# A two-layer trunk step on one core: the first feed-forward projection run tile by tile as its shift and scale columns are computed, with activations and vectors laid out on the host

## What is computed

```python
mod = (silu(cond) @ w_mod[layer] + b_mod[layer]).reshape(-1, 9, 1024)      # 9 vectors of 1024 for each of 2 conditions
# first sub-layer: shift = mod[:,0], scale = mod[:,1], gate = mod[:,2]
h = x * rsqrt(mean(x*x) + 1e-6) * norm_g[0] * (1 + scale) + shift          # cond = c_ctx for context, c for latent
x = x + 0.5 * gate * ((silu(h @ w_gate) * (h @ w_up)) @ w_out)             # FFN width 2816
...                                                                       # mixer, FFN, FFN, mixer, FFN
return x of the context tokens, x of the latent tokens, new_cache_k, new_cache_v
```

## Time and profile before

| | |
|---|---|
| median of 3 runs | 1500.81 us (1499.41 to 1501.71) |
| the profiled execution | 1499.5 us |
| its span | 1497.7 us |
| PE busy, of the span | 94% |
| first matmul of the first projection | 45.47 us |
| start of unit 2 | 67.53 us |
| end of the first FFN's matmuls | about 325.4 us |
| last residual done | about 1489.9 us |

### The profile page before, as it was taken

One profiled execution on the slowest core, in us unless ns is written; L12 is line 12 of the kernel. 1 busy time (PEld: TensorE's weight loads), 2 busy tenths in 40 slices (PEclk: granted clock), 3 DMA queues, 4 the chain that ended last, 5 costly groups with the idle time before them and its releaser, 6 DMA issues.

```text
span 1497.7 us, 21193 instructions
## 1 busy us (share of the span) xinstructions
PE 1407.8 (94%) x8134; PEld 1375.4 (92%) x8134; DVE 970.0 (65%) x1394; ACT 557.7 (37%) x731; POOL 122.5 (8%) x110
## 2 busy tenths in 40 slices
PE   5799999989866899999998999999989989999998
PEld 3799999989845799999998999999989989999998
DVE  2777678968998566666757666679763477444332
ACT  2433332237666443333224333332345343333221
POOL 1000000014555100000001000000021010000000
PEclk9899999989878999999998999999989999999999
DMA  8765655752200235555652555547523325433421
GB/s 325 261 231 176 203 177 200 285 182 96 86 32 29 102 133 201 188 191 174 234 181 85 197 193 185 193 149 295 219 99 134 126 85 186 137 122 130 141 84 42
DMA packets 45114, 242.96 MB, mean 162 GB/s; under 512 B 4997, under 2 KB 6889, under 8 KB 24328
## 3 DMA queue, kind: packets, MB, share of 16 engines
q1 hardware_dynamic: 44464, 241.99, 46.7%
q10 hardware_dynamic: 600, 0.30, 0.1%
HBM read 240.57 MB, written 1.70 MB: 162 GB/s over the span
## 4 chain that ended last, share of the span: by engine, by line
PE 83%; DVE 10%; DMA 2%; ACT 2%; issue 1%; POOL 1%; ACTq 0%; SPq 0%; DVEq 0%; POOLq 0%
PE ps L1185 27%; PE ps L1186 27%; PE ps L1187 27%; DVE conv L974 4%; DVE w_lo L790 1%; DMA conv_rows<-in_conv_w 1%; DVE n_full L876 1%; PE ps L1254 1%; DVE m_raw L812 1%; DVE smax L1039 1%; ACT w_hi L528 1%; DVE a_lo L883 0%; POOL n_acc L453 0%; DMA m_raw<-in_w_pairs 0%; PE ps L1554 0%
## 5 line engine op out<-in xcount | busy, mean ns | idle before, releaser
L1185 PE MATMUL ps<-a_hi,w_hi 128*128 128x384 f32 x1744 | 591.7, 339 | 19.1 <-DVE a_lo L883 14.0
L1186 PE MATMUL ps<-a_lo,w_hi 128*128 128x384 f32 x1744 | 588.5, 337 | 0.0
L1187 PE MATMUL ps<-a_hi,w_lo 128*128 128x384 f32 x1744 | 588.1, 337 | 0.0
L790 DVE TENSOR_TENSOR w_lo<-w_raw,w_hi 128x2048 fp32r<-128x2048 f32 x153 | 352.9, 2306 | 162.3 <-ACT w_hi L528 162.0
L528 ACT ACTIVATE w_hi<-w_raw 128x2048 fp32r<-128x2048 f32 x153 | 292.1, 1909 | 264.7 <-PE ps L1187 200.2
L1185 PEld LDWEIGHTS ps<-a_hi,w_hi 128*128 128x128 f32 x1744 | 332.1, 190 | 23.4 <-issue 10.0
L1186 PEld LDWEIGHTS ps<-a_lo,w_hi 128*128 128x128 f32 x1744 | 332.1, 190 | 0.1
L1187 PEld LDWEIGHTS ps<-a_hi,w_lo 128*128 128x128 f32 x1744 | 331.7, 190 | 0.0
L812 DVE SCALAR_TENSOR_TENSOR m_raw<-m_raw 128x1024 f32<-128x1024 f32 x252 | 296.0, 1220 | 1.0 <-ACT m_raw L589 1.0
L1187 PE MATMUL ps<-h_hi,w_lo 128*128 (+1 forms) x704 | 236.6, 336 | 0.0
L1186 PE MATMUL ps<-h_lo,w_hi 128*128 (+1 forms) x704 | 236.6, 336 | 0.0
(11 more groups left out here) (179 smaller groups left out, 666.2 us busy)
## 6 DMA issues: line engine op xcount, KB each, us to landing
w_raw<-in_w_units SPq DMA_DIRECT2D x153, 1024.0 KB, 5.0
m_raw<-in_w_rows SPq DMA_DIRECT2D x126, 512.0 KB, 3.6
m_raw<-in_w_pairs SPq DMA_DIRECT2D x9, 1024.0 KB, 7.7
out<-x_nat SPq DMA_DIRECT2D x3, 512.0 KB, 3.1
x_nat<-in_x_sample SPq DMA_DIRECT2D x1, 1024.0 KB, 12.5
fourier<-in_k_fourier SPq DMA_DIRECT2D x1, 768.0 KB, 4.4
x_nat<-in_x_prompt SPq DMA_DIRECT2D x1, 512.0 KB, 10.7
m_raw<-in_c_ctx SPq DMA_DIRECT2D x1, 512.0 KB, 5.7
```

Of the source, the lines that this page charges most:

```text
L790: nc.vector.tensor_tensor(w_lo[:, slot(u), :], w_raw[:, slot(u), :], w_hi[:, slot(u), :].bitcast(FP32), ALU.subtract).then_inc(lo_done, 1)
L1185: mm(out, whi, mhi, start=start, stop=False)
L1186: mm(out, whi, mlo, start=False, stop=False)
L1187: return mm(out, wlo, mhi, start=False, stop=stop)
```

## The change

The host now lays out `x` (as `x_cols`, channels on partitions), the two conditions (`cond_cols`), and all bias and norm vectors (`cols_a`, `cols_b`, `conv_cols`), and transposes the output back (`y_cols`). The transposes on PE and their copies go, at the start and at the end. A pair of modulation columns now holds one tile of shift and the same tile of scale, so pair `k` is all that channel tile `k` needs. There are 8 pairs in place of 9, pairs 3 to 7 in buffers of their own (`p_raw`), all loaded with no wait. After tiles 0 and 1, PE interleaves: pair `k + 2`, then channel tile `k` of units 0 and 1 together (12 matmuls), then the columns of pair `k + 2`. Two more modulation tiles are left to DVE, in the output units.

```diff
-FIRST_TILES = MRING * GROUPS_FIRST * PAIR_TILES
+FIRST_TILES = KT * PAIR_TILES
-TILES_OUT = {0: [3, 3] + [2] * 8, ...
+TILES_OUT = {0: [3] * 4 + [2] * 6, ...
 # SP, start
-            sp.dma_start(ident[:], k_ident).then_inc(const_in, 16)
-            sp.dma_start(cond_rows[0:KT, :], c_ctx...); sp.dma_start(cond_rows[KT:2 * KT, :], c[0]...)
-            for b in range(MRING):
-                load_pair(0, b)
-            sp.dma_start(x_nat[:, 0, :], x_prompt[0]); sp.dma_start(x_nat[:, 1:TT, :], x_sample[0]...)
+            sp.dma_start(cond_raw[:], cond_cols).then_inc(cond_in, 16)
+            sp.dma_start(ident[:], k_ident).then_inc(const_in, 16)
+            sp.dma_start(x[:], x_cols).then_inc(x_in, 16)
 # SP, load_ffn(0)
-                    for pair in range(MRING, MRING * GROUPS_FIRST):
-                        if pair == MRING * GROUPS_FIRST - 2:
-                            load_unit(u0)
-                        load_pair(pair // MRING, pair % MRING)
+                    load_pair(0)
+                    load_unit(u0)
+                    load_unit(u0 + 1)
+                    for k in range(1, KT):
+                        load_pair(k)
+                    load_unit(u0 + 2)
+                    sp.wait_ge(mod_used, MRING)        # then the condition rows and the tiles
 # SP, end
-            for tt in range(TT):
-                sp.wait_ge(out_c, tt + 1)
-                sp.dma_start(dst, x_nat[:, tt, :]).then_inc(out_done, 16)
+            for d in range(KT):
+                sp.wait_ge(x_ready, KT * N_SUB + d + 1)
+                sp.dma_start(y_cols[:, d, :], x[:, d, :]).then_inc(out_done, 16)
 # ACT
-            act.wait_ge(cond_t, 1)
+            act.wait_ge(cond_in, 16)
-            for dst, src in ( ... 13 row loads ... (conv_rows[:, :], conv_w[0])):
+            for dst, src in ((vec_a[:], cols_a), (vec_b[:], cols_b), (conv_wt[:], conv_cols)):
                 act.dma_start(dst, src).then_inc(vectors_in, 16)
             norm_stats(0)
-            ...                                        # vec_a, vec_b, conv_wt out of PSUM
             split(0)
-            norm(0)
+            norm(0, 0, 1)
             split(1)
+            norm(0, 1, KT)
 # DVE
+            def part_copy(k):
+                dve.wait_ge(mod_used, k + 1)
+                if k >= 2:
+                    dve.wait_ge(cols_done, k - 1)
+                nc.vector.tensor_copy(mod_part[:, k % 2, :], ps[:, SUM_BANK[k % 2], 0:PAIR]).then_inc(part_copied, 1)
+            def first_modulation(k):
+                dve.wait_ge(cols_done, k + 1)
+                nc.vector.tensor_scalar(m_shift[:, 0, k, :], ps[:, 7, 0:2], vec_a[...], None, ALU.add)
+                nc.vector.tensor_scalar(m_scale[:, 0, k, :], ps[:, 7, 2:4], scale_bias[:, k:k + 1],
+                                        vec_a[...], ALU.add, ALU.mult).then_inc(first_mods, 1)
+            dve.wait_ge(vectors_in, 48)
+            dve.wait_ge(dve_self, mark(nc.vector.tensor_scalar(scale_bias[:], vec_a[...], 1.0, None, ALU.add)))
+            dve.wait_ge(x_in, 16)
+            dve.sem_inc(x_ready, KT)
             part_copy(0)
-            for d in range(KT):
-                dve.wait_ge(x_t, d + 1)
-                nc.vector.tensor_copy(x[:, d, :], ps[:, d % 6, 0:TOK]).then_inc(x_ready, 1)
-            cols_copy(0)
+            first_modulation(0)
             norm_stats(0)
-            part_copy(1); cols_copy(1); split(0); part_copy(2); cols_copy(2); modulation_in(0); norm(0); split(1)
+            dve.wait_ge(bc_done, 1)
+            dve.wait_ge(first_mods, 1)
+            scaled(0, 0)                               # n_full of one tile, the first half of norm()
+            low(0, 0)                                  # a_lo of one tile, the second half
+            split(0)
+            split(1)
+            part_copy(1)
+            first_modulation(1)
+            for k in range(1, KT):
+                dve.wait_ge(first_mods, k + 1)
+                scaled(0, k)
+                if k + 1 < KT:
+                    part_copy(k + 1)
+                low(0, k)
+                if k + 1 < KT:
+                    first_modulation(k + 1)
             ffn(0)
 # PE
+            def mod_sums(k):
+                pe.wait_ge(pair_in[k], 16)
+                if k >= 2:
+                    pe.wait_ge(part_copied, k - 1)
+                ...                                    # 8 matmuls, 128x256 moving, 32 columns each, as before
             pe.wait_ge(cond_ready, 2)
+            mod_sums(0)
+            mod_columns(0)
+            norm_sums(0)
+            norm_spread(0)
+            mod_sums(1)
+            mod_columns(1)
+            for m in range(2):
+                pe.wait_ge(lo_done, RING + m + 1)
+            for k in range(KT):
+                if k + 2 < KT:
+                    mod_sums(k + 2)
+                pe.wait_ge(a_ready, k + 1)
+                for m in range(2):
+                    for h in range(2):
+                        ins = three(ps[:, 2 * m + h, 0:TOK], ..., a_hi[:, k, :], a_lo[:, k, :], k == 0, k == KT - 1)
+                    if k == KT - 1:
+                        ins.then_inc(unit_done, 1)
+                if k + 2 < KT:
+                    mod_columns(k + 2)
             ffn(0)                                     # without its first_units; continues with unit 2
-            ...                                        # at the end: 24 transposes of x; ACT: 3 copies to x_nat
```

More of the change, by code:

```diff
@@ L157, in modulation_pairs, with columns @@
 def modulation_pairs(w_mod):
-    n = MRING * GROUPS_FIRST
-    w = w_mod[0, :, 0:n * PAIR].reshape(KT, P, n, PAIR).transpose(2, 1, 0, 3)
-    return np.ascontiguousarray(w, dtype=np.float32).reshape(n, P, UNIT)
+    w = w_mod[0, :, 0:2 * D_MODEL].reshape(KT, P, 2, KT, P).transpose(3, 1, 0, 2, 4)
+    return np.ascontiguousarray(w, dtype=np.float32).reshape(KT, P, UNIT)
+def columns(*vectors):
+    return np.ascontiguousarray(np.concatenate([np.asarray(v, np.float32).reshape(-1, P) for v in vectors]).T)
 def modulation_rows(w_mod):
@@ L217, in build @@
         n_full = sb("n_full", [P, KT, TOK], stack=r)
[L218 to L221, removed]
+        p_raw = sb("p_raw", [P, KT - MRING, UNIT], stack=r)
         r.close()
@@ L267, in build @@
         unit_done = sem("unit_done")
-        mod_in = [sem(f"mod_in{i}") for i in range(MRING)]
+        pair_in = [sem(f"pair_in{k}") for k in range(KT)]
         mod_used = sem("mod_used")
@@ L540, in norm_stats, with norm @@
                 nc.scalar.activation(stat[:, 4:4 + TT], stat[:, 0:TT], ACT.Sqrt).then_inc(root_done, 1)
-            def norm(n):
-                for d in range(KT):
+            def norm(n, d0=0, d1=KT):
+                for d in range(d0, d1):
                     for cnd, lo, hi in SEGS:
@@ L866, in norm_stats, with scaled, low @@
                                         stat[:, 8:8 + TT].unsqueeze(2).to_broadcast([P, TT, P]), ALU.mult).then_inc(diag_done, 1)
+            def scaled(n, d):
+                for cnd, lo, hi in SEGS:
+                    nc.vector.scalar_tensor_tensor(n_full[:, d, lo:hi], ps[:, BC_BANK[n], lo:hi],
+                                                   m_scale[:, n, d, cnd:cnd + 1], x[:, d, lo:hi],
+                                                   ALU.mult, ALU.mult).then_inc(full_done, 1)
+            def low(n, d):
+                for cnd, lo, hi in SEGS:
+                    dve.wait_ge(a_hi_done, 2 * (KT * n + d) + cnd + 1)
+                    ins = nc.vector.scalar_tensor_tensor(a_lo[:, d, lo:hi], n_full[:, d, lo:hi],
+                                                         m_shift[:, n, d, cnd:cnd + 1],
+                                                         a_hi[:, d, lo:hi].bitcast(FP32), ALU.add, ALU.subtract)
+                ins.then_inc(a_ready, 1)
             def norm(n):
-                bank = BC_BANK[n]
                 dve.wait_ge(bc_done, n + 1)
@@ L1569, in _ @@
             ffn(5)
-            pe.wait_ge(x_ready, KT * (N_SUB + 1))
-            for tt in range(TT):
-                for d in range(KT):
-                    ins = nc.tensor.transpose(ps[:, 2 * tt + d // 4, (d % 4) * P:(d % 4 + 1) * P],
-                                              x[:, d, tt * P:(tt + 1) * P], ident[:])
-                ins.then_inc(out_t, 1)
 FFN_AT = {0: 0, 2: 1, 3: 2, 5: 3}
@@ L1612 @@
     named["w_rows"] = modulation_rows(np.asarray(inputs["w_mod"]))
+    tokens = np.concatenate([np.asarray(inputs["x_prompt"])[0], np.asarray(inputs["x_sample"])[0]])
+    named["x_cols"] = np.ascontiguousarray(tokens.reshape(TOK, KT, P).transpose(2, 1, 0), dtype=np.float32)
+    named["cond_cols"] = columns(inputs["c_ctx"], inputs["c"])
+    vectors = {n: np.asarray(inputs[n]) for n in _VECTORS}
+    named["cols_a"] = columns(vectors["b_mod"][0], vectors["norm_g"])
+    named["cols_b"] = columns(vectors["b_mod"][1], *(vectors[n] for n in _VECTORS[2:7]),
+                              *(np.tile(vectors[n], 2) for n in _VECTORS[7:]))
```

(1 more changed line is left out.)

189 lines of the change are left out of this document (50 added, 139 removed).

## The result

The changed kernel takes 1505.88 us (median of 8 runs, 1504.07 to 1509.38), the kernel before beside it 1501.69 us (8 runs). The ratio is 1.0032, 95% interval 1.0021 to 1.0043: slower by 0.3%, where no change was forecast. The profiled execution's span grew from 1497.7 to 1502.3 us.

A forecast was written before the change was run, and what follows sets the result against it. PE was taken as the bound from unit 2 on, so only unit 2's start and the tail matter. Start 3.8 + clock 1.5 - end 5.2 = +0.1 us, median 1500.81 to 1500.9, range 1494.5 to 1506.

The forecast's parts named there:

- Costed at nothing: Loads ahead of their use, condition rows, and two extra DVE tiles covered in the output units: no cost.
- The bound given for the lost cover: Output units: without cover, the two extra DVE tiles would cost 4.6 us.
- a gap at PE in the output units, which would be the two extra tiles: Listed sign of a wrong forecast: PE waiting in the output units because of DVE's two added tiles; no size given.
- Vectors: Start: all three vector loads landed at 15.7 us, 384 packets at 41 a us on ACT's queue.
- Rival A: Start: vectors arrive early, at best x limits at 8.5, all steps 7.2 us earlier, 1493.7 us; chance 0.20.
- Norm, copy, rounds: Start, after the vectors: squares 16.1, first products 35.9, rounds 3.62 each, last a_hi 58.8, unit 2 at 71.3 us.
- rivals B and C: B: rounds at half clock, up to 19 us more, 0.12; C: late vectors or round waits, from 3.0 us, 0.18.
- Clock: Unit 2, after PE's idle: half clock for 3 us loses 1.5 us, bounds 0 and 3.4.
- rival D: PE's gap before unit 2 leaves clock up, only the end counts: 1499.4 us; chance 0.50 together with the forecast.
- The end: After the last residual: last store lands in 1.9 us, span ends at 1492.5, gain 5.2 us (4.4 to 5.5).
- the 2.45 us of the prediction: Kernel's end: the last store's landing time by the skill's fit, which would make the gain 4.7 us.

The follow-up runs named there:

- experiment 2: Kernel before with two more modulation tiles in the first FFN's output units, two fewer in the second's: 1506.27 us, ratio 1.0024 to the kernel before.
- experiment 1: Changed kernel with its two extra modulation tiles moved from the output units to right after step(0): 1503.39 us, ratio 1.0005 to the kernel before.
- experiment 3: Changed kernel with unit 33 loaded before the first FFN's last two modulation tiles in SP's queue: 1500.29 us, ratio 0.9985 to the kernel before.
- experiment 6: Changed kernel with x released as it lands, DVE waiting first only for vec_a: 1500.36 us, ratio 0.9985 to the kernel before.

## Why the prediction was wrong

**The step that failed** is the one under "Costed at nothing": "The two extra DVE tiles fall in the output units. There the split of unit 26 is done at 260.2 and needed at 267.0". The cover was measured at the split, which indeed stayed early: PE has no gap from unit 2 to 332. It was not measured at the end of DVE's queue, where gate and residuals stand. There DVE had no cover already before: its gate came at 322.36, 3.4 us before the end of PE's last product, with 16 residuals of 0.33 us behind it (5.3 in all), and PE waited 2.31. The bound given for the lost cover, 4.6 us, holds the 3.3 us of the border. The tiles cost 3.6 us alone (experiment 2) and give about 4 back when taken out of the change (experiment 1). Part of the path was not seen at all: the lateness passes through SP's queue, as tile, free buffer, load of unit 33, split, and then the gate (experiment 3). The prediction's list of signs did name this one: "a gap at PE in the output units, which would be the two extra tiles". The gap came just behind those units.

**Vectors.** 15.7 was worked out and 15.77 measured, but that close a match is luck. ACT's queue moved 432 packets from 6 to 16 us, not 384, and 54 a us and not 41 (the rows below):

```profile
q1 hardware_dynamic: 378, 2.74, 93.6%
q10 hardware_dynamic: 378, 0.15, 7.9%
```

(After, 7 to 14 us: packets, MB, share; q1 is SP's queue, q10 ACT's.) With these two figures the prediction's sum, 2.7 + 3.5 + 432/54, would have been 14.2. Rival A was right that full rows go faster than the mean rate of before, and wrong that the vectors would be early by much. The Trainium skill says in "DMA: Bandwidth & Descriptors", section "Queues, rings and completion order", that a DMA engine drains a whole packet of one ring, typically some 9 to 17 descriptors, before it switches. By the prediction's reading of it, the 8 rows of a load on each engine would have gone in one turn. The trace does not agree: the two queues moved 378 packets each in 7 us, one for one, and the counts keep within 3 of each other in single stretches of 0.2 us too (7.2 to 7.8 us: 9 to 10, 11 to 12, 14 to 13). Waiting for all three loads cost 7.0 us by ratio (experiment 6; 5.8 by landmarks), near the 7.2 that the prediction gave rival A at best.

**Norm, copy, rounds.** Squares at 16.06 (16.1), first products at 36.52 (35.9), the five rounds after the first 3.64 each (3.62) without a wait, so rivals B and C are out. The spread took 1.65 in place of 1.35, the copy of pair 1's sums started at 33.24 in place of 32.5, and the first 12 matmuls took 2.93 in place of 2.6. With such tenths the last `a_hi` is at 59.91, 1.1 later than 58.8, and unit 2 at 72.49, 1.2 later than 71.3.

**Clock.** 3.1 us at half clock in unit 2 (windows above), 1.46 us longer to the FFN's end: as sized. (Its upper bound, 3.4 for "twice as long at half", should be 3.0.) So rival D did not come.

**The end** gave 5.56 for 5.2. The last store landed in 1.9 us, as in proportion. The fit in the Trainium skill's "DMA: Bandwidth & Descriptors", section "Anatomy of one DMA", is given there for DMAs that GpSimd issues, and SP issues these stores, so the 2.45 us of the prediction stretched it, and the trace does not agree with it.

**In sum**, +0.1 was forecast. With 3.3 for the border and 1.2 for the start it would have been +4.6. The measured ratio stands for +3.2 to +6.5. The time of 1505.88 us lies within the stated range of 1494.5 to 1506 at its upper end, but the change was clear of noise, and it was slower for a reason that none of the rivals had.

## What to carry to other kernels

Cover for work added to an in-order queue is to be read at the last thing that the queue owes before the stage ends, not only at the next thing it owes. Follow it through other engines' queues too: a load that nobody waits for soon can stand behind one that waits for the late engine. A gap whose releaser is an elementwise step is a question to ask of the kernel before as well: here its 2.31 us seem to be the visible part of some 4 (13.3 us of border against 9.1 in experiment 3 and 9.35 at the second FFN; not tested on the kernel before by itself). And where data that only a later step needs is waited for together with data for the first, splitting the wait may be worth more than the change at hand (here 7 us of 1506).

## What the runs showed of the hardware that was not expected

A small load on ACT's queue beside the large ones on SP's goes slowly for its size: 60 KB in 128 rows in 8.0 us, while 1536 KB of `x` issued at about the same time landed in 6.7. From 7 to 14 us each queue moved 378 packets, ACT's of 0.4 KB on average, SP's of 7.2 KB. The small rows kept the pace of the large ones, so here a small load's time went by its number of rows and not by its bytes. The issues after:

```profile
x<-in_x_cols SPq DMA_DIRECT2D x1, 1536.0 KB, 6.7
...
vec_a<-in_cols_a ACTq DMA_DIRECT2D x1, 60.0 KB, 8.0
```

The same 18 small matmuls of a norm's sums take 2.5 us at full clock right behind products (experiment 3), 3.95 us behind a gap of 2.31 (kernel before) and 4.2 us behind one of 5.62 (changed kernel). Such a gap is paid twice, once as a wait and once in the work behind it.
